# Block attention's gates and branch products turned to tokens on the partitions, fixed PSUM banks, state sums ahead of a head norm, and a last block in two steps

## The reference, cut to what matters

```
u = rms_norm(x) @ w_in            # gq gk gv g_lr g_r | mq mk mv | gate_a gate_b
# gated linear attention, chunks of 64 tokens, 4 heads
kv    = kl^T v  per chunk;  S_n = decay_n * S_(n-1) + kv_n     # states, summed in order
o_a   = rms_norm(qd S_prev + tril(qd kd^T) v) * silu(g_r);  y_a = o_a @ w_branch_a
# block attention, 8 heads of 128, all 256 tokens are one block
y_b   = softmax(rms(mq) rms(mk)^T * s - slope*distance, causal) @ mv @ w_branch_b
y     = sigmoid(gate_a) * y_a + sigmoid(gate_b) * y_b;   x = x + y @ w_out
...
x     = x + sigmoid(rms_norm(x) @ w_ple_gate) * (p @ w_ple)    # the output
```

## Time and profile before

| | |
|---|---|
| median of 3 runs | 1430.96 us (1430.71 to 1434.16) |
| profiled execution: time, span | 1433.57 us, 1431.8 us |
| TensorE matmul busy | 1270.9 us, 89% of the span |
| VectorE, ScalarE busy | 949.8 us (66%), 596.8 us (42%) |
| mean granted TensorE clock | 0.977 |
| gather of the experts | about 285 to 900 us, DMA-bound |
| second block | about 915 to 1432 us |

### The profile page before, as it was taken

The page is one execution under the profiler, slowest core; times in us unless marked ns, Lnnn a source line. Parts: engine busy times, 40 slices in busy tenths (PEclk is TensorE's granted clock), DMA queues, the critical chain, the costliest instruction groups (busy, mean ns, idle before and its releaser), DMA issues.

```text
span 1431.8 us, 15935 instructions
## 1 busy us (share of the span) xinstructions
PE 1270.9 (89%) x5802; PEld 887.0 (62%) x5802; DVE 949.8 (66%) x1977; ACT 596.8 (42%) x1052; POOL 274.6 (19%) x281
## 2 busy tenths in 40 slices
PE   7989998988787878888787777899999999999998
PEld 7878897534343433434243223597689898888887
DVE  5757556877777777777776776655565556876445
ACT  5656453323123232322222223564446744555344
POOL 1000001443434434343434433000000000000000
PEclk9999998799999999999999999999999999999999
DMA  7432533999999999999999999554254354545551
GB/s 279 177 133 89 176 118 143 406 421 421 422 420 422 421 421 420 422 421 422 420 421 417 422 422 421 219 180 149 102 188 148 118 177 177 184 177 199 186 203 59
DMA packets 56981, 398.76 MB, mean 278 GB/s; under 512 B 7096, under 2 KB 7352, under 8 KB 9032
## 3 DMA queue, kind: packets, MB, share of 16 engines
q0 software_dynamic: 36864, 268.45, 45.1%
q1 hardware_dynamic: 17856, 125.84, 24.4%
q10 hardware_dynamic: 2184, 3.45, 0.7%
HBM read 396.67 MB, written 1.05 MB: 278 GB/s over the span
## 4 chain that ended last, share of the span: by engine, by line
PE 55%; DMA 25%; DVE 9%; ACT 7%; issue 3%; POOL 1%; ACTq 0%; SPq 0%; DVEq 0%
PE ps L781 35%; DMA B<-in_ex,eidx 24%; PE ps L1117 9%; PE ps L809 4%; DVE B L2409 3%; ACT hl L1364 2%; PE ps L810 2%; DVE hl L1931 2%; ACT diags L1631 1%; DMA ring<-in_wt 1%; POOL B L745 1%; ACT L1620 1%; ACT av_ L1624 1%; PE ps L1026 0%; PE ps L1008 0%
## 5 line engine op out<-in xcount | busy, mean ns | idle before, releaser
L1117 PE MATMUL ps<-B,diags 128*128 128x512 f32 x1024 | 484.7, 619 | 122.8 <-ACT diags L1631 122.8
L1117 PEld LDWEIGHTS ps<-B,diags 128*128 128x128 f32 x1024 | 189.8, 195 | 390.9 <-ACT diags L1631 195.2
L2409 DVE CUSTOM_DVE_ANT_0 B<-B 128x1024 f32<-128x1024 f32 x256 | 311.8, 1222 | 120.7 <-DMA B<-in_ex,eidx 120.5
L1931 DVE TENSOR_TENSOR hl<-ring,hl 128x2048 fp32r<-128x2048 f32 x116 | 265.5, 2290 | 188.8 <-ACT hl L1364 188.6
L745 POOL DMA_INDIRECT B<-in_ex,eidx x256 | 268.6, 1049 | 615.5 <-PE ps L1117 362.7
L1364 ACT ACTIVATE hl<-ring 128x2048 fp32r<-128x2048 f32 x116 | 221.5, 1911 | 108.0 <-PE ps L781 105.1
L1624 ACT ACTIVATE av_<-av_ 128x2 f32<-128x2 f32 x128 | 26.0, 203 | 431.8 <-DVE av_ L2409 431.8
L781 PE MATMUL ps<-XT,hl 128*128 128x256 f32 x1344 | 182.7, 294 | 0.7 <-DVE XT L1940 0.7
L781 PE MATMUL ps<-hl,R 128*128 128x512 f32 x768 | 178.7, 392 | 0.3 <-DVE R L1947 0.3
L781 PEld LDWEIGHTS ps<-XT,hl 128*128 128x128 f32 x1344 | 168.2, 193 | 15.2 <-issue 14.0
L781 PEld LDWEIGHTS ps<-hl,R 128*128 128x128 f32 x768 | 143.0, 188 | 30.7 <-DVE R L1947 0.7
(11 more groups left out here) (354 smaller groups left out, 977.0 us busy)
## 6 DMA issues: line engine op xcount, KB each, us to landing
ring<-in_wt SPq DMA_DIRECT2D x117, 1024.0 KB, 4.8
B<-in_ex,eidx POOLq DMA_INDIRECT x256, 13.6
X<-in_x SPq DMA_DIRECT2D x2, 512.0 KB, 4.3
B<-in_mem ACTq DMA_DIRECT2D x1, 1024.0 KB, 10.3
ring<-in_wple SPq DMA_DIRECT2D x1, 1024.0 KB, 4.7
out<-B SPq DMA_DIRECT2D x4, 256.0 KB, 2.0
GB<-in_gffn ACTq DMA_DIRECT2D x1, 512.0 KB, 3.8
GB<-in_gfin ACTq DMA_DIRECT2D x1, 512.0 KB, 10.5
```

The source lines that it names most:

```text
L1117: m = e.matmul(acc[tb][hf][:, :], diags[:, i % 4, :], rows[i % NG][:, 1024 + 512 * hf:1536 + 512 * hf], start=(s == 0), stop=(s == 127))
L1931: e.tensor_tensor(w[1][:, :], ring[:, i % RING, :], w[0][:, :].bitcast(F32), ALU.subtract).then_inc(lo.sem)
L2409: m = e.tensor_tensor_reduce(R[:, 0:1024], R[:, 0:1024], XG[:, tb, :], 1.0, 0.0, ALU.mult, ALU.add, av_[:, tb, s + z:s + z + 1])
```

## The change

Four parts.

1. **Linear attention.** TensorE does half bq(0,1) ahead of the states of chunks 0 and 1. ScalarE splits half 49 only, copies klT, and then splits half 50; its square root for the head norm and the second gate's silu come ahead of the splits of 51 and 52. VectorE sums the states of chunks 0 and 1 first, then does the head norm, then the split of half 51; it no longer splits half 52 between.
2. **Gates and branches.** ga, gb, wa and wb become form "t". Sigmoids and products work on 128 x 512 pieces with tokens on the partitions, both pieces of a layer after its second half, so in the rounds with odd h only. The sum y then has tokens on the partitions, and TensorE turns it with 16 transposes in four groups `yT`, two of them inside wb 1 and two inside wo2 0; ScalarE and VectorE split the turned pieces from PSUM, not from SBUF.
3. **Banks.** In the stage every group has a fixed bank: scores of even and odd heads on 4 and 5, all transposed probabilities on 6, all value products on 7.
4. **The last block.** The last of the four groups of pg is cut into two of 256 columns (12 matmuls of 512 columns become 24 of 256 in each half), each with its own sigmoid, product, sum and output DMA.

Tables and banks:

```diff
- ("gr", 2, "t"), ("bq", 2, "t"), ("bk", 2, "t"), ("bv", 2, "t"), ("ga", 2, "f"), ("gb", 2, "f"), ("wa", 2, "f"),
- ("wb", 2, "f"), ("wo2", 2, "t"), ("up", 8, "f"), ("dn", 8, "t"), ("pg", 2, "t")]
+ ("gr", 2, "t"), ("bq", 2, "t"), ("bk", 2, "t"), ("bv", 2, "t"), ("ga", 2, "t"), ("gb", 2, "t"), ("wa", 2, "t"),
+ ("wb", 2, "t"), ("wo2", 2, "t"), ("up", 8, "f"), ("dn", 8, "t"), ("pg", 2, "t")]
...
+LAST = [(0, 0, 0, 512), (0, 1, 0, 512), (1, 0, 0, 512), (1, 1, 0, 256), (1, 1, 256, 256)]
...
-SGA, SGB, yT = feat(Bf[4]), feat(Bf[6]), feat(Bf[5])
+SGA, SGB, yg = pair(Bf[4]), pair(Bf[6]), pair(Bf[5])
...
+tmp = pair(Bf[8])
 yR = [feat(Br[j]) for j in (2, 3)]
...
+for i, (name, k) in enumerate((("ga", 0), ("gb", 0), ("ga", 1), ("gb", 1), ("wa", 0), ("wa", 1))):
+    FIXED.update({(name, k, tb): (2 * (i % 2) if i else 6) + tb for tb in range(2)})
+for h in range(8):
+    FIXED.update({("mS", h): 4 + h % 2, ("mPT", h): 6, ("mV", h // 2): 7})
+for tb in range(2):
+    FIXED.update({("wb", 0, tb): tb, ("wb", 1, tb): 4 + tb, ("yT", tb): 6 + tb, ("wo2", 0, tb): 2 * (1 - tb),
+                  ("wo2", 1, tb): 1 + 6 * tb, ("yT", 2 + tb): 3 + 3 * tb})
 BANK, holder, turn = {}, {}, 0
```

TensorE:

```diff
+    t_half("bq", 0, 1, XT)
     e.wait_ge(*klts[1])
...
         for n in range(2):
             mark(m[n], ("SA", n, hp))
-    t_half("bq", 0, 1, XT)
...
         if name == "wa":
-            f_half(name, k, h, oT2, [lo_part["oN", j] for j in range(4)] if k + h == 0 else None)
+            t_half(name, k, h, oT2, [lo_part["oN", j] for j in range(4)] if k == 0 else None)
         else:
-            f_half(name, k, h, XT)
+            t_half(name, k, h, XT)
 
...
+
+    def turn_branches(j):
+
+        ps = bank(("yT", j))
+        for tb in range(2):
+            e.wait_ge(*wbs[j // 2, tb])
+            for kk in range(2):
+                o = kk * 256 + tb * 128
...
+
     for k in range(2):
         for h in range(2):
-            f_half("wb", k, h, mT_, [lo_part["m", j] for j in range(4)] if k + h == 0 else None)
-    for h in range(2):
-        t_half("wo2", 0, h, yR, [lo_part["y", j] for j in range(4)])
+            t_half("wb", k, h, mT_, [lo_part["m", j] for j in range(4)] if k == 0 else None)
+            if (k, h) == (1, 0):
+                for j in range(2):
+                    turn_branches(j)
+    yt = [lo_part["y", j] for j in range(4)]
+    t_block("wo2", 0, 0, 0, yR, yt)
+    for j in range(2, 4):
+        turn_branches(j)
+    mark(t_block("wo2", 0, 0, 1, yR), ("used", NUM["wo2", 0, 0]))
...
         flip("x4T", j, "dn")
-    for k in range(2):
-        for h in range(2):
-            t_half("pg", k, h, XT, [lo_part["x4", j] for j in range(4)] if k == 0 else None)
+    for h in range(2):
+        t_half("pg", 0, h, XT, [lo_part["x4", j] for j in range(4)])
+    for h in range(2):
+        n = NUM["pg", 1, h]
+        e.wait_ge(*lo[n])
+        w = [p[:, :].rearrange("p (k n) -> p k n", k=4) for p in PARTS[n]]
+        for i, (_, tb, o, c) in enumerate(LAST[2:]):
+            ps = bank(("pg", 1, i)) if h == 0 else ps_of(("pg", 1, i))
+            m = prod(ps[:, 0:c], lambda a, k: XT[a][:, k, tb * 128:tb * 128 + 128],
+                     lambda b, k: w[b][:, k % 4, o:o + c], range(4 * h, 4 * h + 4), h == 0, h == 1)
+            if h:
```

ScalarE:

```diff
     gate_r(0)
-    split_to(n + 5)
+    split_to(n + 4)
     for tb in range(2):
         e.wait_ge(*pe["klT", tb])
         e.activation(klt[:, tb * 512:tb * 512 + 512], ps_of(("klT", tb))[:, :], ACT.Copy).then_inc(klts.sem)
+    split_to(n + 5)
     squares(0)
+    sqrt(("bn", 0))
     split_to(n + 6)
-    sqrt(("bn", 0))
+    gate_r(1)
     split_to(n + 7)
...
     def gated(i):
         name, k, h = GATED[i]
-        if name != "wa":
-            e.wait_ge(*pe[GATED[i]])
+        if name != "wa" and h:
             dst = SGA if name == "ga" else SGB
-            e.activation(dst[:, 4 * k + 2 * h:4 * k + 2 * h + 2, :], half_ps(GATED[i]),
-                         ACT.Sigmoid).then_inc((gas if name == "ga" else gbs).sem)
+            for tb in range(2):
+                e.wait_ge(*pe[name, k, tb])
+                e.activation(dst[:, tb, k * 512:k * 512 + 512], ps_of((name, k, tb))[:, :],
+                             ACT.Sigmoid).then_inc((gas if name == "ga" else gbs).sem)
         split_to(NUM[GATED[i]] + 3)
...
     for k in range(2):
         for h in range(2):
-            c = 4 * k + 2 * h
-            part(("y", 2 * k + h), yR[0][:, c:c + 2, :], yT[:, c:c + 2, :], wbs[k, h])
             split_to(NUM["wb", k, h] + 3)
+            if k == 1:
+                for j in range(2 * h, 2 * h + 2):
+                    part(("y", j), yR[0][:, 2 * j:2 * j + 2, :], half_ps(("yT", j)), pe["yT", j])
...
-            e.activation(SG[:, tb, k * 512:k * 512 + 512], ps_of(("pg", k, tb))[:, :], ACT.Sigmoid,
-                         scale=norm["x4"][0][:, tb:tb + 1]).then_inc(pgs.sem)
+    for k, tb, o, n in LAST:
+        e.wait_ge(*pe["pg", k, tb + o // 256])
+        e.activation(SG[:, tb, k * 512 + o:k * 512 + o + n], ps_of(("pg", k, tb + o // 256))[:, 0:n], ACT.Sigmoid,
+                     scale=norm["x4"][0][:, tb:tb + 1]).then_inc(pgs.sem)
     assert parted[0] == len(HALVES)
 
```

VectorE:

```diff
-        if n < 2:
-            split_to(51 + n)
-        if n == 0:
+        if n == 1:
             head_norm(0)
+            split_to(51)
     gate_r(1)
...
     def gated(i):
         name, k, h = GATED[i]
-        if name == "wa":
-            c = slice(4 * k + 2 * h, 4 * k + 2 * h + 2)
-            e.wait_ge(*pe[GATED[i]])
-            e.wait_ge(*gas[k, h])
-            e.tensor_tensor(yT[:, c, :], half_ps(GATED[i]), SGA[:, c, :], ALU.mult).then_inc(was.sem)
+        if name == "wa" and h:
+            c = slice(k * 512, k * 512 + 512)
+            for tb in range(2):
+                e.wait_ge(*pe[name, k, tb])
+                e.wait_ge(*gas[k, tb])
+                e.tensor_tensor(yg[:, tb, c], ps_of((name, k, tb))[:, :], SGA[:, tb, c], ALU.mult).then_inc(was.sem)
         split_to(NUM[GATED[i]] + 3)
...
-        for h in range(2):
-            c = slice(4 * k + 2 * h, 4 * k + 2 * h + 2)
-            e.wait_ge(*pe["wb", k, h])
-            e.wait_ge(*gbs[k, h])
-            e.tensor_tensor(tmp[:, c, :], half_ps(("wb", k, h)), SGB[:, c, :], ALU.mult).then_inc(wbm.sem)
-            e.wait_ge(*wbm[k, h])
-            e.tensor_tensor(yT[:, c, :], yT[:, c, :], tmp[:, c, :], ALU.add).then_inc(wbs.sem)
-            part(("y", 2 * k + h), yR, c, yT[:, c, :])
-            split_to(NUM["wb", k, h] + 3)
+        c = slice(k * 512, k * 512 + 512)
+        split_to(NUM["wb", k, 0] + 3)
+        if k == 1:
+            for j in range(2):
+                part(("y", j), yR, slice(2 * j, 2 * j + 2), half_ps(("yT", j)))
+        for tb in range(2):
+            e.wait_ge(*pe["wb", k, tb])
+            e.wait_ge(*gbs[k, tb])
+            e.tensor_tensor(tmp[:, tb, c], ps_of(("wb", k, tb))[:, :], SGB[:, tb, c], ALU.mult).then_inc(wbm.sem)
+            e.wait_ge(*wbm[k, tb])
+            e.tensor_tensor(yg[:, tb, c], yg[:, tb, c], tmp[:, tb, c], ALU.add).then_inc(wbs.sem)
+        split_to(NUM["wb", k, 1] + 3)
+    for j in range(2, 4):
+        part(("y", j), yR, slice(2 * j, 2 * j + 2), half_ps(("yT", j)))
     n = NUM["wo2", 0, 0]
     split_to(n + 4)
...
-            e.tensor_tensor(y, y, X[:, tb, k * 512:k * 512 + 512], ALU.add).then_inc(pgo.sem)
+    for k, tb, o, n in LAST:
+        c = slice(k * 512 + o, k * 512 + o + n)
+        y = SG[:, tb, c]
+        e.wait_ge(*pgs[k, tb, o, n])
+        settle(e.tensor_tensor(y, y, PW[:, tb, c], ALU.mult))
```

More of the change, by code:

```diff
@@ L317, in program @@
         pws = count("pws", [(tb, h) for tb in range(2) for h in range(2)])
-        pgs = count("pgs", [(k, tb) for k in range(2) for tb in range(2)])
+        pgs = count("pgs", LAST)
         ulo = count("ulo", [(k, h) for k in range(8) for h in range(2)])
@@ L357, in program @@
         qns = count("qns", [(j, tb) for j in range(4) for tb in range(2)])
-        was = count("was", [(k, h) for k in range(2) for h in range(2)])
+        was = count("was", [(k, tb) for k in range(2) for tb in range(2)])
         mor = count("mor", range(8))
@@ L665, in program @@
         MARKS += [("x4T", 2), ("x4T", 3)]
-        for k in range(2):
-            for h in range(2):
-                t_marks("pg", k, h)
+        for h in range(2):
+            t_marks("pg", 0, h)
+        MARKS += [("used", NUM["pg", 1, 0]), ("pg", 1, 0), ("pg", 1, 1), ("pg", 1, 2)]
         pe = count("pe", MARKS)
```

66 lines of the change are left out of this document (35 added, 31 removed).

## The result

The changed kernel takes 1417.61 us (median of 4, 1417.39 to 1418.8), the kernel before beside it 1430.84 (4 runs, 1430.18 to 1434.16). The ratio is 0.9905, with a 95% interval of 0.9892 to 0.9919: 13.2 us less, a change of 0.95% that is clear of the noise, where 15 were forecast (1416, range 1412.5 to 1424). Over all runs of the study the medians are 1431.5 (54 runs) and 1418.0 (8), which is 13.5. The profiled execution took 1418.8, its span 1417.1. Lines have moved: the product helper L781 of before is L799 now, the states' L1181 is L1199.

A forecast was written before the change was run, and what follows sets the result against it. TensorE was taken as the bound, with pauses and slow clock in linear attention and a ScalarE-VectorE ring in block attention's first rounds. Gains 10.1 + 4.5 + 0.6 = 15.2 off the median 1430.96 gave 1416 us, range 1412.5 to 1424.

The forecast's parts named there:

- the cover: Linear attention: TensorE has other work while it would wait, 4 us at the first pause, 3 us at the second.
- so 10.1 us are lost: Linear attention, bq(0,0) to bT: 37.0 us against 26.9 of work at full pace; pauses of 2.16 and 3.10, rest slow clock.
- The -5.3 of the working before its last step: Block attention: 5.1 earlier at head 5's values, 2.1 from seven cheaper halves, less 1.9 for 16 new transposes.
- Rounds of 6.26 and 8.74: Block attention's ring between ScalarE and VectorE: even-h rounds fall from 8.14 to 6.26, odd-h rounds take 8.74.
- I set 0.8 for what is not: Block attention: loss from TensorE's waits on single banks 6 and 7 and the clock, beyond waiting it would do anyway.
- The last block: -0.6: End of kernel: shorter sigmoid, product and sum give -0.85, the cut matmul group costs +0.15 twice; bounds 0 and 1.2.
- The wait between wb and wo2: Second transposes of y: turned pieces ready 5.8 us behind wb's end, wanted at 6.3; half a microsecond of cover.
- The rule against the row: Block attention's table loads: the skill adds 1380 ns drain per switch, worth another 5.5 us; the row shows 1.28 only.
- Locked rounds: Rival, 1420 us, chance 0.18: single banks hold TensorE to the ring, clock falls behind pauses, block attention gains nothing.
- moved pauses: Rival, 1423 us, chance 0.10: a later linear attention wait replaces one pause, 5 us return, block attention gains 2.
- No change: Rival, 1431 us, chance 0.05: something the trace does not name, such as the weights' DMA, holds the pauses.
- Half clock throughout: Rival, 1454 us, chance 0.05 with other losses above 4.3: pauses drop the clock every block attention round, 12.4 against 8.14.

The follow-up runs named there:

- a third: Trace of the changed kernel with the linear attention's change taken back (gates, branches, banks and last block stay changed): 1425.51 us, ratio 0.9964 to the kernel before.

## Why the prediction was right, and where not

**Linear attention: mechanism right, term too large.** Both pauses went, the cover held at both places, nothing late took their place, and the clock stayed at its higher level: 9.8 in the traces against 10.1 forecast. The step that was mis-sized is "so 10.1 us are lost", as a term to be taken off the median. It took the clock loss of one execution as the kernel's own. Beside 27.2 of work and the pauses' 5.26, which repeat, the clock took 4.4 to 4.6 in two traces and 1.9 in a third. The prediction itself says that its execution was 2.6 above the median; that this is the same 2.6 is likely, not shown, since the start alone wanders by 2.8. Counted from an execution like the third, the term is 7.2, and 7.2 + 5.3 + 0.6 = 13.1, where 13.2 was measured. The interval of the ratio (11.6 to 15.5 us) holds this sum and the forecast one of 15.2. The runs of the parts speak for both sizes, 7.0 when the linear attention is changed last and 8.9 when it is changed alone, so how large the term is in the median stays open between 7 and 9.

**Block attention: -4.5 forecast, -5.3 measured.** The -5.3 of the working before its last step came out. Rounds of 6.26 and 8.74 were forecast; the quoted ones were 6.24 and 8.64. The last exponential comes 5.8 earlier (5.7). The values of head 5 start 64.3 behind the first scores where they started 69.2 behind, 4.9 earlier (5.1), and behind them another 0.4 is gained (0.2). The step that failed is "I set 0.8 for what is not": six waits were expected, three of 1.8 to 1.9, and a fallen clock. There were three in the rounds, 0.28, 0.92 and 1.12, and no fall. The single banks cost nothing by themselves: with tanh, on the same banks, TensorE does not wait in the rounds at all.

That the total came nearer than its largest term has luck in it: one term was too large and the other too small.

**The last block: -0.6, right.** From the last sigmoid to the last sum 0.75 less, where 0.85 was reckoned: the sigmoid of 256 columns took 0.47, and the 0.38 had been read from a copy. The rest of the span 0.64 less, which also has the cut matmuls in it.

**The wait between wb and wo2** did not come: wo2 has no bracket in the timeline. It starts 24 matmuls of 0.228 behind 1175.25, at 1180.7, which is 105.7 behind the first scores and was 111.9 before, and the second group of transposes then takes 0.9 of these 6.2 back.

**The rule against the row.** The row was right. Had each switch cost another 1.38 us of drain, the rounds without one would have been 3.26 shorter than those of before, not 1.9. In the changed kernel too the sigmoid follows its load at once (1103.40 + 1.28 to 1104.69), and the load follows the exponential's last record at once (1103.19 + 0.19 to 1103.40), so there is no drain on either side. The Trainium skill ("ScalarE: Activation LUTs", What ACT_TABLE_LOAD costs) has that drain for every switch; no trace here shows it.

**The rivals.** *Locked rounds* and *moved pauses* did not come: 122.93 and 27.18 with brackets as above. *No change* is out by the interval of the ratio. *Half clock throughout* did not come either: read in steps of 5 us, no window of block attention was below 1.00. How near it was, the sigmoid in every round tells: there one pause reached 2.00 us and the clock fell to 0.56 for 3.5 us. The Trainium skill ("TensorE: Matmul & The Clock Gate", A second HAM failure mode) describes small idle times between groups that bring the clock down; here no pause of up to 1.12 us in the rounds did.

## What to carry to other kernels

Read the clock loss behind a pause as a thing of that execution, not of the kernel. Where the profiled execution stands above the median of the runs, ask which term holds the difference before you take the whole of it off. A loop that two engines hand to each other is costed by its chain, start to start, and a table load on that chain costs its own 1.28 us; a function from the set already loaded (tanh for a sigmoid, between exponentials) removes it. A semaphore that is named at a wait tells where the wait is seen: move it, and see whether time falls or only the name changes.
